# Gated DeltaNet scan: both triangles of the block inverses in one VectorE chain, R fused, the state's decay on ScalarE, prologue reordered

## The reference

```python
m = jnp.where(strict, jnp.einsum('bhncd,bhnsd->bhncs', kb, k) * decay, 0.0)
a = m + jnp.eye(DN_CHUNK, dtype=m.dtype)
u = lax.linalg.triangular_solve(a, v * beta[..., None], ...)
w = lax.linalg.triangular_solve(a, kb * jnp.exp(gc)[..., None], ...)
...
def step(s, inp):
    qd, kd, ui, wi, ai, gl = inp
    v_new = ui - jnp.einsum('bhck,bhkv->bhcv', wi, s)
    o = jnp.einsum('bhck,bhkv->bhcv', qd, s) + jnp.einsum('bhcs,bhsv->bhcv', ai, v_new)
    s = s * jnp.exp(gl)[..., None, None] + jnp.einsum('bhck,bhcv->bhkv', kd, v_new)
    return s, o
```

## Time and profile before

| | us |
|---|---|
| timed runs, median of 3 | 3703.55 (3703.0 to 3704.4) |
| profiled execution, own time | 3708.23 |
| its span in the trace | 3706.4 |
| PE busy in the span | 3473.9 |
| DVE busy | 1830.5 |
| ACT busy | 990.3 |
| POOL busy | 875.8 |

### The profile page before, as it was taken

The page is one execution under the profiler, slowest core; times in us unless marked ns, Lnnn a source line. Parts: engine busy times, 40 slices in busy tenths (PEclk is TensorE's granted clock), DMA queues, the critical chain, the costliest instruction groups (busy, mean ns, idle before and its releaser), DMA issues. The chain is left out here.

```text
span 3706.4 us, 41570 instructions
## 1 busy us (share of the span) xinstructions
PE 3473.9 (94%) x15660; PEld 2202.6 (59%) x15660; DVE 1830.5 (49%) x2771; ACT 990.3 (27%) x1973; POOL 875.8 (24%) x874
## 2 busy tenths in 40 slices
PE   6999998789989998789999999999969999999998
PEld 2445443789985444444444444445558788788786
DVE  4454544677665553462222222234356666656666
ACT  4365556133334320221111111112201111111113
POOL 1022222565555400201011111123321212222211
PEclk9999999799999999999999999999959999999999
DMA  8222332556554413951111221134335656566566
GB/s 291 72 78 79 94 100 70 157 173 198 172 191 140 133 46 116 310 164 42 57 57 57 94 68 57 40 120 149 124 127 199 207 198 217 187 217 197 186 216 250
DMA packets 354831, 523.44 MB, mean 141 GB/s; under 512 B 50236, under 2 KB 225887, under 8 KB 354441
## 3 DMA queue, kind: packets, MB, share of 16 engines
q1 hardware_dynamic: 331316, 462.06, 37.2%
q0 software_dynamic: 12096, 43.84, 4.5%
q10 hardware_dynamic: 11221, 14.87, 1.1%
HBM read 410.85 MB, written 111.97 MB: 141 GB/s over the span
## 5 line engine op out<-in xcount | busy, mean ns | idle before, releaser
L2837 POOL TENSOR_TENSOR mg<-mg,sg_m 128x512 f32<-128x512 f32 x64 | 98.1, 1533 | 777.3 <-DVE sg_m L2718 777.3
L3724 PE MATMUL bank<-xeT,raw_e 128*128 128x128 f32 x2304 | 267.9, 275 | 0.8 <-ACT xeT L3568 0.8
L3724 PEld LDWEIGHTS bank<-xeT,raw_e 128*128 128x128 f32 x2304 | 263.6, 192 | 8.3 <-issue 8.3
L2624 PE MATMUL bank<-hT,raw_w 128*128 128x512 f32 x576 | 261.6, 597 | 5.2 <-PEq L2428 5.2
L957 POOL TENSOR_SCALAR sg<-tmp 128x512 f32<-128x512 f32 (+1 forms) x76 | 113.4, 1493 | 427.2 <-DVE tmp L1025 367.0
L2624 PEld LDWEIGHTS bank<-hT,raw_w 128*128 128x128 f32 x576 | 110.3, 192 | 144.2 <-issue 144.2
L3724 PE MATMUL bank<-T_e,U 128*128 128x128 f32 x1536 | 176.7, 275 | 0.0
L3724 PEld LDWEIGHTS bank<-T_e,U 128*128 128x128 f32 x1536 | 174.1, 192 | 0.0
L2624 PE MATMUL bank<-zT,S 128*128 128x512 f32 x384 | 172.6, 592 | 0.0
L685 PE MATMUL bank<-T_d,S_d 128*128 128x512 f32 x384 | 171.5, 593 | 0.0
L2718 DVE TENSOR_TENSOR sg_m<-sg_m,bank 128x512 f32<-128x512 f32 x64 | 43.9, 686 | 228.1 <-PE bank L2636 228.1
(11 more groups left out here) (540 smaller groups left out, 7145.2 us busy)
## 6 DMA issues: line engine op xcount, KB each, us to landing
raw_e<-in_exp_w_gate SPq DMA_DIRECT2D x16, 3072.0 KB, 16.5
raw_e<-in_exp_w_up SPq DMA_DIRECT2D x16, 3072.0 KB, 12.8
raw_e<-in_exp_w_down SPq DMA_DIRECT2D x16, 3072.0 KB, 10.3
raw_w<-in_w_in SPq DMA_DIRECT2D x24, 1024.0 KB, 5.7
raw_d<-in_w_in SPq DMA_DIRECT2D x16, 1024.0 KB, 5.9
raw_h<-in_w_in SPq DMA_DIRECT2D x12, 1024.0 KB, 5.3
x0T<-in_ada_w SPq DMA_DIRECT2D x44, 256.0 KB, 3.1
raw_h<-kT_d SPq DMA_DIRECT2D x36, 256.0 KB, 5.4
```

The lines of the kernel that those rows point to most:

```text
L2624: mm = pe.matmul(bank[:, :], lhs[:, k, :], rhs[:, k, :], start=first and k == 0, stop=k == 3, skip_group_check=not first)
L2837: pool.tensor_tensor(mg[:, i, :], mg[:, i, :], sg[:, i, :], ALU.add).then_inc(add_ok[i], 1)
L3724: mm = pe.matmul(bank[:, f * P:(f + 1) * P], lhs[:, k, f * P:(f + 1) * P], rhs[:, k, :], start=fresh and k == 0, stop=k == 3, skip_group_c ...
```

## The change

- The two triangles of a pair's blocks are solved by one chain, `solve`, on DVE. Its partitions 0 to 63 are the lower triangles; partitions 64 to 127 hold the same blocks turned, so that the upper triangles become lower ones. The blocks are loaded twice (`nb` and `raw_u`), turned by a copy at the chain's start and turned back by one at its end; with the unit copy that is 32 instructions. POOL has no chain left.
- In an even step both halves of the chain run behind R. The odd steps hold none, and in the prologue only the chain of pair 0 stands ahead of the first step; that of pair 1 has moved into step 0.
- R is one fused operation for each head on DVE, product times the negated decay (`negc`) plus the values. POOL's subtraction is gone.
- The decay of S is eight activations on ACT, behind the first turned copy of the merge (`turned(m, 0)`).
- Prologue: the products of fronts 0 and 1 are grouped (both differences, then key products, then query products), POOL's mask of front 3 waits for the chain of pair 0, merging waits for three fronts and no longer for four, and the state products of step 0 stand between the merge levels.

```diff
-            Tb = sbt(st, "Tb", [64, 2, 2, 256])
-            shared = gm[0:64, :, :].rearrange("p k c -> p (k c)")
+            Tb = sbt(st, "Tb", [P, 2, 2, 256])
+            negc = sbt(st, "negc", [P, NCH, 8])
+            shared = gm[:, :, :].rearrange("p k c -> p (k c)")
...
+            raw_u = [shared[64:128, 512 + r * 256:512 + (r + 1) * 256] for r in range(2)]
+            prod, unit = sbt(st, "prod", [P, 64]), shared[:, 1024:1280]
...
+            INV = 3 + 2 * (ROWS - 2) + 1
...
+            def solve(eng, b, half):
+                x, t, n = nb[b % 2], Tb[:, b % 2, 0, :], [b * INV + (0 if half == 0 else 3 + 2 * (HALF - 1))]
...
+                    link(eng.tensor_copy(t, unit))
+                    link(eng.tensor_copy(grid(x[64:128, :]), turned_grid(raw_u[b % 2])))
+                    link(eng.tensor_scalar(grid(t)[:, 1:ROWS, 0], x[:, 1:ROWS], -1.0, None, ALU.mult))
+                for k in (range(1, HALF) if half == 0 else range(HALF, ROWS - 1)):
+                    area = [P, ROWS - 1 - k, k + 1]
+                    work = prod[:, 0:(ROWS - 1 - k) * (k + 1)].rearrange("q (i c) -> q i c", c=k + 1)
+                    link(eng.tensor_tensor(work, x[:, k * ROWS + k + 1:(k + 1) * ROWS].unsqueeze(2).to_broadcast(area), grid(t)[:, k:k + 1, 0:k + 1].to_broadcast(area), ALU.mult))
+                    link(eng.tensor_tensor(grid(t)[:, k + 1:ROWS, 0:k + 1], grid(t)[:, k + 1:ROWS, 0:k + 1], work, ALU.subtract))
+                if half == 1:
+                    link(eng.tensor_copy(grid(Tb[64:128, b % 2, 1, :]), turned_grid(t[64:128, :])))
...
                             sp.dma_start(nb[b % 2][32 * w:32 * w + 32, :]..., padded(nc_d[f])[:, :, 0:ROWS]).then_inc(nb_in[b % 2], 16)
+                            sp.dma_start(raw_u[b % 2][32 * w:32 * w + 32, :]..., padded(nc_d[f])[:, :, 0:ROWS]).then_inc(nb_in[b % 2], 16)
...
+                    def decayed_state(s, d):
+                        act.wait_ge(q_mm, nth(s, d))
+                        act.wait_ge(s_ok, nth(s, d))
+                        for h in heads:
+                            last = act.activation(S[:, d, h, :], S[:, d, h, :], ACT.Copy, scale=column(etot, s, d, h))
+                        last.then_inc(sx_ok, 1)
...
-                    def difference_to_values(s, d):
-                        pool.wait_ge(r1_ok, nth(s, d))
-                        pool.tensor_tensor(R[:, d], vN[:, s % 2, d], R[:, d], ALU.subtract).then_inc(r_ok, 1)
...
-                    dve.wait_ge(lv_in, 32)
+                    dve.tensor_scalar(negc[:, :, :], egc[:, :, :], -1.0, None, ALU.mult).then_inc(neg_ok, 1)
...
                     def rest(s, d):
                         dve.wait_ge(k_mm, nth(s, d))
-                        dve.tensor_tensor(R[:, d], b4(4 + 2 * d), per_token(egc, s, d), ALU.mult).then_inc(r1_ok, 1)
+                        dve.wait_ge(ldv[s % 2], 64 * (s // 2 + 1))
+                        for h in heads:
+                            last = dve.scalar_tensor_tensor(R[:, d, h, :], b4(4 + 2 * d)[:, h, :], column(negc, s, d, h), vN[:, s % 2, d, h, :], ALU.mult, ALU.add)
+                        last.then_inc(r_ok, 1)
...
                         rest(s, 0)
                         rest(s, 1)
                         if s % 2 == 0 and s + 2 < STEPS:
-                            lower_blocks((s + 2) // 2, 1)
+                            solve(dve, (s + 2) // 2, 0)
+                            solve(dve, (s + 2) // 2, 1)
...
-                        if s % 2 and ahead:
-                            lower_blocks((s + 3) // 2, 0)
```

More of the change, by code:

```diff
@@ L1402, in output @@
                         mm4(4 + 2 * d, attn(s, d), V[:, d]).then_inc(out_mm, 1)
-                    for f in range(AHEAD):
+                    differences(0)
+                    differences(1)
+                    for f in range(2):
+                        for d in range(2):
+                            key_product(f, d)
+                    for f in range(2):
+                        for d in range(2):
+                            query_product(f, d)
+                    for f in range(2, AHEAD):
                         differences(f)
@@ L1409, in _ @@
                             query_product(f, d)
+                    pe.wait_ge(nc_ok, AHEAD - 1)
+                    merge_inner(0, 0)
+                    merge_outer(0, 0)
                     pe.wait_ge(at_ok, nth(AHEAD - 1, 1))
-                    for l in range(NL):
-                        merge_inner(0, l)
-                        merge_outer(0, l)
+                    merge_inner(0, 1)
+                    key_state(0, 0)
+                    merge_outer(0, 1)
+                    key_state(0, 1)
+                    merge_inner(0, 2)
+                    query_state(0, 0)
+                    merge_outer(0, 2)
+                    query_state(0, 1)
                     for s in range(STEPS):
@@ L1509, in _ @@
                             turned(m, 0)
+                        for d in range(2):
+                            decayed_state(s, d)
+                        if m < STEPS:
                             for l in range(1, NL):
@@ L1541, in _ @@
[L1541 to L1563, removed]
-                            work = prod_b[:, 0:k * (ROWS - k)].rearrange("q (i c) -> q i c", c=ROWS - k)
-                            link(pool.tensor_tensor(work, x[:, k * ROWS:k * ROWS + k].unsqueeze(2).to_broadcast(area), grid(t)[:, k:k + 1, k:ROWS].to_broadcast(area), ALU.mult))
-                            link(pool.tensor_tensor(grid(t)[:, 0:k, k:ROWS], grid(t)[:, 0:k, k:ROWS], work, ALU.subtract))
@@ L1682, in front @@
                             attention(f, d)
-                    for f in range(AHEAD - 1):
-                        front(f)
-                    lower_blocks(0, 0)
-                    lower_blocks(0, 1)
+                    for f in range(2):
+                        for d in range(2):
+                            gram(f, d)
+                        gram_sum(f)
+                    for f in range(2):
+                        for d in range(2):
+                            attention(f, d)
+                    front(2)
+                    solve(dve, 0, 0)
+                    solve(dve, 0, 1)
                     front(AHEAD - 1)
```

89 lines of the change are left out of this document (34 added, 55 removed).

## The result

| | before, us | changed, us | ratio, 95% interval |
|---|---|---|---|
| timed side by side, 20 runs each | 3705.23 (3699.4 to 3716.2) | 3713.41 (3706.4 to 3720.7) | 1.0019 (1.0011 to 1.0027) |
| profiled execution, own time | 3708.23 | 3713.44 | |
| its span | 3706.4 | 3711.6 | |

The interval of the ratio lies wholly above 1, at 4 to 10 us: a small slowdown is measured. It is at the edge of the 0.2%, 7.4 us, that the forecast counted as no change, and 3713 stands inside its range of 3694 to 3717. The medians are 8.2 us apart; the forecast had +2.7. So the mechanism has to be looked at step by step, and the missing 5.5 us with it.

The account below looks back on a forecast made before the run. PE was taken as the bound in odd steps, DVE's leaving the chain in even steps. Prologue -3.9, even steps +3.0 and +1.9, step 14 0, tail +1.7 gave +2.7 us: 3706 by the timed median, range 3694 to 3717.

Parts of the forecast that it names:

- What bounds an even step: Even steps of the scan: the moment at which DVE leaves the chain sets their length; R is a lesser wait.
- Part 1: One chain for both triangles: a solve without company takes 8.05 us, with turned copies at 0.45 us.
- Part 2: Even steps: six links held, E at K + 16.5 against 15.87, one PE wait of 4.5 us, none for R.
- 3.0 + 1.9: Even steps: +0.6 us in each of steps 2 to 10, together +3.0, and +1.9 in step 12.
- the 0: Step 14: E comes 1.5 us earlier, but one wait of 4.6 us with the lower clock behind it: 0.
- Part 3: Decay on ScalarE: eight activations take 2.2 us, cost 0 in odd steps, +1.7 us from step 15 on.
- Part 4: Prologue: merging begins 4.6 us earlier, and E of the first step comes at 719.6, against 723.49.
- -3.9 us: Prologue's term in the sum, with PE at full clock by 711.9; bounds -7 and +0.5.
- The first step's E: Sign in the changed profile, at the prologue's end: E of the first step at 717 to 722.
- the prologue gains nothing: Rival, prologue: the clock stays down while it merges, 3710.5 us, still no change; chance 0.15.
- Slower, DVE and POOL hold each other: Rival, between R and E of even steps: links hold POOL too, E 1.4 us later, 3717 us; chance 0.24.
- Faster, by the clock: Rival, even steps: one long wait brings no clock fall, seven steps gain 1.5 us each, 3695.5 us; chance 0.14.

Follow-up runs that it names:

- e4: The changed kernel with POOL's gates and keys held back in even steps until the solve ends: 3681.83 us, ratio 0.9935.
- e5: The changed kernel with only POOL's keys held back in even steps until the solve ends: 3701.93 us, ratio 0.9995.
- e6: The changed kernel with the state's decay back on POOL, ahead of the masks: 3729.41 us, ratio 1.0065.
- e3: The changed kernel with the prologue's old order on all engines: 3710.84 us, ratio 1.0018.
- e1: The changed kernel timed again without an edit: 3711.13 us, ratio 1.0012.
- e11: The kernel of e10 with the prologue's old order on all engines: 3659.35 us, ratio 0.988.
- e10: The kernel of e8 with the state's decay back on POOL for steps 15 and 16 alone: 3662.47 us, ratio 0.9886.
- e7: The kernel before with the fused R on DVE alone, solve and decay as before: 3682.72 us, ratio 0.994.
- e8: The kernel of e4 with the solve cut in three pieces, k = 1 to 8 ahead of E: 3659.38 us, ratio 0.9883.
- e9: The kernel before with the fused R and the state's decay on ScalarE, both solves as before: 3680.70 us, ratio 0.9937.

## Why the prediction was right or wrong

*What bounds an even step*: right. The step's length hangs on the moment at which DVE leaves the solve; e4, e5 and e6 move that moment and the time goes with it.

*Part 1*: right. Without company the solve took 8.1 us in the prologue, for 8.05. The turned copies took 0.38 and 0.37 us, below the 0.45 chosen and within its bounds. The estimate of 0.8 us by the Trainium skill's figure (Vector Engine (DVE) Microarchitecture Reference, section 5.2) is twice what the rows show. The figure of 2.5 ns alone gives an estimated 0.64 us for 256 columns, and it stands there for both sources or the destination stepping 24 words, not for a copy with a stepping source alone.

*Part 2*: right in mechanism and nearly in size. Six held links; E at K + 16.2 for K + 16.5; one wait, of 5.6 us for 4.5, since it was counted from K + 12 and PE had run out of work a little earlier; none for R. Steps 2 to 12 grew by 4.2 us between the first two profiles and by 4.8 between the second, for 3.0 + 1.9. That the sum fits so well is in part luck: E itself came 0.3 to 0.4 us later in steps 4 to 10, for 0.6, and single steps grew by -0.1 to +1.6 in the first pair, with the clock. Step 12 lasts 29.4 to 29.6 us, for 29.9; but before, the short step was another one in the second profile (step 2 with 27.9 us, step 12 with 29.5). The wait of 5.6 us is outside the 4 to 5 that the forecast named as a sign. Step 14 took 25.9 and 24.4 against 24.7, so the 0 is open by about a microsecond.

*Part 3*: right. The eight activations took 2.43 us, for 2.2. Steps 15 and 16 went from 18.25 to 18.77 us, 0.52 each for 0.55, and the scan's end behind the last transpose from 14.0 to 14.6, for 0.6. The odd steps didn't change.

*Part 4*: **the step that failed**, the term "-3.9 us". The new order is worth nothing that the runs can tell: without it e3 is 0.3 us below e1 by the medians and 2 us above it by the ratios, and e11 is 3.1 us below e10. Its price was taken from one execution in which PE merged at the lower clock, and the forecast let the changed kernel have the full one. E of the first step did come earlier (715.4, for 719.6), but 715.4 against 723.5 is mostly this difference in clock; in the second profiles E comes 72.5 us into the stage before and 75.3 in the changed kernel. Up to the end of step 0 the changed kernel is 7.0 us ahead in the first pair of profiles and 5.4 behind in the second, so no single pair could have priced this term. The first step's E was named as a sign, at 717 to 722: it came at 715.4 in the first profile and at 719.1 in the second. The rival "the prologue gains nothing" had the cause half right and the outcome fully: 3710.5, +7.0, where 3711 to 3713, or +6 to +8, was measured.

With that term at 0 the sum is +6.6 us, which fits both measurements.

*The rivals.* Slower, DVE and POOL hold each other: it fell. POOL's six instructions took 2.53, 2.03 and 2.03 us a pair, without a gap, in the step shown, and one link was held for each, six as forecast; without links beside them the masks took 2.50 and the gates 2.04 (e4, behind the solve). Faster, by the clock: the clock didn't stay up in the changed kernel, but e7 and e8 in all six even steps 2 to 12, e9 in five of them and e4 in two show that it can. That is worth 1.4 us a step in e4, 1.6 in e9, and 1.8 between the kernel before and e7.

What the forecast didn't see, though its total wasn't hurt by it: the near zero is a gain of some 23 us and a loss of some 30. It put half the links on the other side of R and noted that the gain "is paid back", but never asked what R beside the masks, with half the links done, would give. Nor did it see that POOL's own chain had kept gates and keys off DVE's links.

## What to carry to other kernels

When a change with several parts comes out near zero, time the parts alone: here one of them was worth 22 us and another cost 30. Count what stands beside what: in these runs each 128x512 GpSimd instruction held one of the small dependent VectorE operations on SBUF, so either let GpSimd's work fall beside VectorE operations that read from the matmul banks, or hold it back until the chain is through. And don't price a prologue from one profile in which the matmul engine's clock happened to be low; profile the kernel before twice.

## What the runs showed of the hardware

- Which DVE operations are held: the links (both inputs in SBUF) took 0.96 to 1.20 us in the steps shown beside a 128x512 POOL instruction (0.80 in e9, where that one had run for 0.5 us when the link started) and 0.17 to 0.23 without; R (first input in a matmul bank, second in SBUF) took 2.16 us for eight beside two masks and 2.15 to 2.16 without. This agrees with the condition in the Trainium skill (SBUF — State Buffer, the list under the diagram of the ports: a DVE operation "with two SBUF inputs" and a GpSimd one that reads SBUF). Its lock, which makes the other one wait whoever comes first, is seen here in one direction only: DVE waits, and in the steps read POOL's pairs grew by 0.06 us at most (masks 2.50 without links, 2.52 to 2.56 beside them). In e6 an operation with one input, the first column of 128x15, was held too:

```profile
867.40 2.04 POOL L1595 TENSOR_TENSOR S<-S,etot 128x512 f32<-128x512 f32 x2 [12.27 <-PE bank L1346]
867.50 0.98 DVE L1217 TENSOR_SCALAR Tb<-gm 128x15 f32<-128x15 f32 x1
868.51 0.97 DVE L1221 TENSOR_TENSOR prod<-gm,Tb 128x28 f32<-128x28 f32 x1
```

- Short POOL instructions hold less: beside POOL's own links DVE's took 0.28 to 0.36 us, all but a few of the smallest, instead of 0.17 to 0.22 (e7).
- Waits of PE cost more than their length. Two waits of 2.1 and 0.7 us left the clock at 1.00 (e7); one of 2.7 us lowered it in some steps and not in others (e4), and so did 0.4 and 2.1 us, in one step of six (e9); one of 4.2 us (e5) or 5.6 us (e1) lowered it in every step, to a mean of 0.88 to 0.94.
- Twice the partitions cost a link nothing that shows: 0.22 us for 128x60 against 0.21 to 0.22 for 64x60.
